# Gated multiplies on another engine, waits of GpSimd taken away, and a reordered weighting in the token mixer of a hybrid layer

## The reference, cut to what matters

```python
# one layer, SEQ = 2048 tokens, D_MODEL = 1024, 4 differential heads, 4 HGRN2 heads
proj = rms_norm(x, g) @ w_in                       # q k v | q f i g
# differential attention, swept over blocks of 128 queries, block-causal in chunks of 64
p = softmax(where(mask, q_blk @ k.T, -inf))        # two maps per head
w = p[0] - lam * p[1]
od = rms_norm(w @ v, subln_g) * (1 - lam_init)
# HGRN2, chunkwise: decayed causal scores inside a chunk, a state between chunks
o = scores @ v_c + (q_c * exp(b_c)) @ state
state = exp(b_last) * state + (k_c * exp(b_last - b_c)).T @ v_c
orr = rms_norm(o, hgrn_norm_g) * silu(g)
x = x + concat(od, orr) @ w_out
x = x + (silu(h @ w_gate) * (h @ w_up)) @ w_down   # h = rms_norm(x)
```

## Time and profile before

| | |
|---|---|
| median of 3 runs | 2812.81 us (2812.19 to 2814.52) |
| profiled execution | 2812.81 us |
| its span, first to last instruction | 2811.1 us |
| PE, PEld busy | 2643.0 us (94%), 2235.6 us (80%) |
| DVE, ACT, POOL busy | 1495.4, 1106.0, 756.8 us |
| mean granted TensorE clock | 0.973 of full |

### The profile page before, as it was taken

One profiled execution on the slowest core, in us unless ns is written; L12 is line 12 of the kernel. 1 busy time (PEld: TensorE's weight loads), 2 busy tenths in 40 slices (PEclk: granted clock), 3 DMA queues, 4 the chain that ended last, 5 costly groups with the idle time before them and its releaser, 6 DMA issues. The chain is left out here.

```text
span 2811.1 us, 34114 instructions
## 1 busy us (share of the span) xinstructions
PE 2643.0 (94%) x13384; PEld 2235.6 (80%) x13384; DVE 1495.4 (53%) x1887; ACT 1106.0 (39%) x1871; POOL 756.8 (27%) x527
## 2 busy tenths in 40 slices
PE   7999999995999999987995999999999997999999
PEld 6888888885888888875884888887888885888887
DVE  5434343431676767653336656657656554446643
ACT  4434343331567666673234222224222222423221
POOL 5000000001524242300003554455544542146400
PEclk9999999997999999998997999999999998999999
DMA  4545455455443433206656333335433333787763
GB/s 162 197 165 180 135 179 177 153 180 151 114 106 106 106 106 83 76 16 202 211 179 216 98 113 98 99 105 197 113 98 98 102 112 96 254 291 253 254 212 126
DMA packets 338672, 415.78 MB, mean 148 GB/s; under 512 B 18512, under 2 KB 212048, under 8 KB 336720
## 3 DMA queue, kind: packets, MB, share of 16 engines
q1 hardware_dynamic: 338512, 413.60, 47.1%
HBM read 291.38 MB, written 122.16 MB: 147 GB/s over the span
## 5 line engine op out<-in xcount | busy, mean ns | idle before, releaser
L1850 PE MATMUL gate_bank<-gate_b_hi,gate_a_hi 128*128 128x512 f32 x1232 | 482.8, 392 | 35.6 <-DVE first_b_lo L1730 21.6
L1852 PE MATMUL gate_bank<-gate_b_hi,gate_a_lo 128*128 128x512 f32 x1232 | 481.7, 391 | 0.0
L1851 PE MATMUL gate_bank<-gate_b_lo,gate_a_hi 128*128 128x512 f32 x1056 | 412.6, 391 | 0.0
L1850 PEld LDWEIGHTS gate_bank<-gate_b_hi,gate_a_hi 128*128 128x128 f32 x1232 | 232.9, 189 | 86.4 <-issue 22.6
L1852 PEld LDWEIGHTS gate_bank<-gate_b_hi,gate_a_lo 128*128 128x128 f32 x1232 | 232.8, 189 | 48.6
L2128 PE MATMUL down_prod<-down_w_hi,down_f_hi 128*128 128x512 f32 x616 | 241.3, 392 | 20.1 <-DVE down_f_lo L2064 19.1
L525 PE MATMUL proj_prod<-proj_w_hi,proj_h_hi 128*128 128x512 f32 x640 | 253.0, 395 | 6.8 <-DVE proj_w_lo L380 6.1
L380 DVE TENSOR_TENSOR proj_w_lo<-proj_w_raw,proj_w_hi 128x2048 fp32r<-128x2048 f32 x56 | 128.8, 2300 | 230.1 <-ACT proj_w_hi L280 230.1
L527 PE MATMUL proj_prod<-proj_w_hi,proj_h_lo 128*128 128x512 f32 x640 | 250.1, 391 | 0.0
L526 PE MATMUL proj_prod<-proj_w_lo,proj_h_hi 128*128 128x512 f32 x640 | 249.9, 390 | 0.0
L2129 PE MATMUL down_prod<-down_w_lo,down_f_hi 128*128 128x512 f32 x616 | 240.6, 391 | 0.0
(11 more groups left out here) (212 smaller groups left out, 5569.7 us busy)
## 6 DMA issues: line engine op xcount, KB each, us to landing
proj_w_raw<-in_w_in_dram SPq DMA_DIRECT2D x56, 1024.0 KB, 6.5
first_full<-in_w_gate_dram SPq DMA_DIRECT2D x88, 256.0 KB, 4.0
gate_full<-in_w_up_dram SPq DMA_DIRECT2D x88, 256.0 KB, 4.0
ff<-gate_ff_sum SPq DMA_DIRECT2D x88, 256.0 KB, 2.9
down_w_raw<-in_w_down_dram SPq DMA_DIRECT2D x22, 1024.0 KB, 7.5
down_f_raw<-ff SPq DMA_DIRECT2D x56, 384.0 KB, 3.3
down_f_raw<-ff SPq DMA_DIRECT2D x56, 320.0 KB, 3.4
gate_b_lo<-operands SPq DMA_DIRECT2D x12, 1024.0 KB, 9.8
```

The source lines that it names most:

```text
L1850: pe.matmul(dst, a_hi[:, pos, s, :], b_hi[pos][:, s, :], start=opens and s == 0, stop=False, skip_group_check=True)
L1851: pe.matmul(dst, a_hi[:, pos, s, :], b_lo[pos][:, s, :], start=False, stop=False, skip_group_check=True)
L1852: last = pe.matmul(dst, a_lo[:, pos, s, :], b_hi[pos][:, s, :], start=False, stop=s == HALF_SLABS - 1, skip_group_check=True)
```

## The change

Four places of `mix_tokens` are edited. (1) GpSimd's running products of a head are made at the head's beginning, all seven, behind the gate product of the head before. (2) GpSimd no longer waits for `combined`, neither in the levels nor in front of the gate product. (3) The recurrence's chunks 4 to 7 are normalised by VectorE, one instruction of 128x512 with a broadcast scale each, at the end of the step in which ScalarE did it; behind the last step ScalarE first normalises the attention's four chunks in a row, and then takes the chunks. (4) `behind` is gone: groups 0 and 1 are always weighed in the step in which they are turned.

```diff
-    def behind(s):
-        return 1 if groups_of(s) == 3 else 2
...
 # GpSimd
             for h in range(HEADS):
-                if h == 0:
-                    pool.wait_ge(rf_in, 16)
-                    for m in range(LEVELS):
-                        product(h, m)
+                pool.wait_ge(rf_in, 16 * (h + 1))
+                for m in range(LEVELS):
+                    ...
+                    if m:
+                        pool.wait_ge(whole_made, h * LEVELS + m)
+                    nc.gpsimd.tensor_tensor(whole[m + 1][:], src[:, :, 0], src[:, :, 1], ALU.mult).then_inc(whole_made, 1)
...
                 for m in range(LEVELS):
                     for side in range(2):
-                        n = fill_at("level", side, m)
-                        pool.wait_ge(fill_done, filled(h, n))
-                        behind_combination(h, n)
+                        pool.wait_ge(fill_done, filled(h, fill_at("level", side, m)))
...
-                if h + 1 < HEADS:
-                    pool.wait_ge(k_ready[1], (h + 1) * LEVELS)
-                    pool.wait_ge(q_ready[1], (h + 1) * UPDATES)
-                    pool.wait_ge(rf_in, 16 * (h + 2))
-                    for m in range(LEVELS - 1):
-                        product(h + 1, m)
-                    pool.wait_ge(fill_read, filled(h, len(FILLS) - 1))
-                    product(h + 1, LEVELS - 1)
-                gate(h)
+                pool.wait_ge(rgate_in, 16 * (h + 1))
+
+                pool.wait_ge(fill_read, filled(h, len(FILLS) - 1))
+                nc.gpsimd.tensor_tensor(ro[:], ro[:], rgate[:], ALU.mult).then_inc(r_gated, 1)
...
 # ScalarE: the branch of normalise() for c >= TURNS is gone (16 instructions of 128x128 a head)
                 if s == TOTAL + 1:
-                    normalise(HEADS - 1, 0)
+                    for c in range(TURNS):
+                        normalise(HEADS - 1, c)
                 for head, c in chunks_at(s):
-                    if s == TOTAL + 1 and c + 1 < CHUNKS:
-                        normalise(head, c + 1)
                     take_chunk(head, c)
                 for head, c in chunks_at(s + 1) if s < TOTAL else ():
-                    normalise(head, c)
+                    if c < TURNS:
+                        normalise(head, c)
...
 # VectorE
+            def normalise(h, c):
+                if c >= TURNS:
+                    dve.wait_ge(r_rrms_made, h + 1)
+                    dve.wait_ge(r_gated, h + 1)
+                    head = c - TURNS
+                    out = ro[:, :, head * C:(head + 1) * C]
+                    scale = ro_rrms[:].rearrange("p (c h) -> p c h", h=HEADS)[:, :, head]
+                    nc.vector.tensor_tensor(out, out, scale.unsqueeze(2).to_broadcast([P, CH, C]), ALU.mult).then_inc(r_scaled, 1)
...
+                for head, c in chunks_at(s + 1) if s <= TOTAL - 1 else chunks_at(s):
+                    normalise(head, c)
...
 # TensorE
-                    pe.wait_ge(r_scaled, (h * HEADS + c - TURNS + 1) * CH)
+                    pe.wait_ge(r_scaled, h * HEADS + c - TURNS + 1)
...
-                    for g in range(behind(s - 2), groups_of(s - 2)):
+                    for g in range(2, groups_of(s - 2)):
                         weigh(s - 2, g)
...
-                    if g < behind(s - 1):
+                    if g < 2:
                         weigh(s - 1, g)
```

More of the change, by code:

```diff
@@ L828, in _ @@
         def _(pool):
-            def product(h, m):
-                src = whole[m][:] if m else rf[:].rearrange("p h n -> p (h n)")
-                src = src.rearrange("p (n s) -> p n s", s=2)
-                if m:
-                    pool.wait_ge(whole_made, h * LEVELS + m)
-                nc.gpsimd.tensor_tensor(whole[m + 1][:], src[:, :, 0], src[:, :, 1], ALU.mult).then_inc(whole_made, 1)
-            def behind_combination(h, n):
-                step = h * STEPS + n // 2
-                if n % 2 == 0 and step:
-                    pool.wait_ge(combined, step)
-            def gate(h):
-                pool.wait_ge(rgate_in, 16 * (h + 1))
-                pool.wait_ge(fill_read, filled(h, len(FILLS) - 1))
-                if h + 1 < HEADS:
-                    pool.wait_ge(combined, (h + 1) * STEPS - 1)
-                nc.gpsimd.tensor_tensor(ro[:], ro[:], rgate[:], ALU.mult).then_inc(r_gated, 1)
-            for h in range(HEADS):
-                if h == 0:
-                    pool.wait_ge(rf_in, 16)
-                    for m in range(LEVELS):
-                        product(h, m)
+            for h in range(HEADS):
+                pool.wait_ge(rf_in, 16 * (h + 1))
+                for m in range(LEVELS):
+                    src = whole[m][:] if m else rf[:].rearrange("p h n -> p (h n)")
+                    src = src.rearrange("p (n s) -> p n s", s=2)
+                    if m:
+                        pool.wait_ge(whole_made, h * LEVELS + m)
+                    nc.gpsimd.tensor_tensor(whole[m + 1][:], src[:, :, 0], src[:, :, 1], ALU.mult).then_inc(whole_made, 1)
                 for side in range(2):
@@ L933, in normalise @@
             def normalise(h, c):
-                if c < TURNS:
-                    act.wait_ge(o_rrms_made, h + 1)
-                    for t in range(c * GROUP, (c + 1) * GROUP):
-                        nc.scalar.activation(o_all[h % 2][:, t, :], o_all[h % 2][:, t, :], ACT.Copy, scale=o_rrms[:, t:t + 1]).then_inc(o_normed, 1)
-                else:
-                    act.wait_ge(r_rrms_made, h + 1)
-                    act.wait_ge(r_gated, h + 1)
-                    head = c - TURNS
-                    for t in range(CH):
-                        part = ro[:, t, head * C:(head + 1) * C]
-                        at = t * HEADS + head
-                        nc.scalar.activation(part, part, ACT.Copy, scale=ro_rrms[:, at:at + 1]).then_inc(r_scaled, 1)
+                act.wait_ge(o_rrms_made, h + 1)
+                for t in range(c * GROUP, (c + 1) * GROUP):
+                    nc.scalar.activation(o_all[h % 2][:, t, :], o_all[h % 2][:, t, :], ACT.Copy, scale=o_rrms[:, t:t + 1]).then_inc(o_normed, 1)
             act.wait_ge(chain, 2)
```

## The result

The changed kernel takes 2838.47 us (median of 4 runs, 2837.49 to 2840.85) against 2812.5 us (2811.06 to 2814.52) for the kernel before on the same chip: a ratio of 1.0093, 95% interval 1.0076 to 1.011, some 26 us slower. The forecast was 17 us slower, 2829.8, in a range of 2816 to 2845. The direction and the range held. The 26 us lie just above the 10 to 24 to which the prediction gave 0.60, and the forecast was 9 us too low.

The account below looks back on a forecast made before the run. TensorE's order of work was taken to bound a head, other engines mattering where it stands for them. Weighing +7.2, head ends +6.6, levels +2.4, chunks +4.2, tail -3.4 summed to +17.0 us: 2829.8, range 2816 to 2845.

Parts of the forecast that it names:

- 10 to 24: Whole kernel: the forecast case, slower by this many us, chance 0.60; the forecast's own times are 2823 to 2837.
- (4) the weighing: Steps 10 to 13: 0.89 us moved ahead of the first scores, partly filling slack; 1.8 us a head, +7.2 us.
- ends of the heads: Three head ends: the early GpSimd products hold VectorE's combination, L1008 ends 2.2 us late each time; +6.6 us.
- levels, steps 7 and 8's combinations: Without its wait GpSimd's k or q can precede L1008; 0.6 us a head on the path, +2.4 us.
- chunks, steps 4 and 5, clock aside: VectorE's normalisations may stand for GpSimd's k and q and make L1008 late; +4.2 us, between 0 and 12.6.
- tail: Behind the last step: ScalarE's chain shortens, six turns of 1.15 us pacing copies; gain 3.4 us, bounds 4.9 and 1.
- The rival that it is free: Steps 10 to 13: the moved weighing costs nothing, leaving +9.8 us, 2822.6; chance 0.10.
- a lateness of all that is left of the other instruction: VectorE against GpSimd: the loser is late by the other's whole remainder; L1004 in step 9 late by 0.23 of 0.45.
- one collision a head: Steps 7 and 8: one of two close races lost per head, 0.6 us left on the path; +2.4 us.
- The rival that both hold it, 2850: Every collision is held by both k and q: levels cost 14, chunks 12.6, sum +37 us; chance 0.15.
- a third of 12.6: Chunks, ends of steps 4 and 5: share taken of the upper bound 3 x 2 x 2.1 us, giving +4.2.
- The rival in which ScalarE is the bound, 2793: ScalarE's queue, not TensorE's, sets a head's length, so 19.6 us come off; chance 0.04.

Follow-up runs that it names:

- experiment 1: Only the moved weighing, group 1 weighed in the step in which it is turned, on the kernel before: 2820.43 us, ratio 1.0024.
- experiment 2: Only the early running products and the gate product without its wait, on the kernel before; levels still wait: 2819.94 us, ratio 1.0018.
- experiment 3: Only the levels' GpSimd wait for the combination removed, on the kernel before: 2818.75 us, ratio 1.0019.
- experiment 4: Only chunks 4 to 7 normalised by VectorE, all GpSimd waits kept, on the kernel before: 2809.4 us, ratio 0.9988.
- experiment 5: The changed kernel with the levels' GpSimd wait for the combination put back: 2822.86 us, ratio 1.0035 to the kernel before.
- experiment 6: Levels without their wait and chunks on VectorE together, on the kernel before; weighing and head ends as before: 2827.9 us, ratio 1.0053.
- Experiment 8: The changed kernel plus 8 unused identity matmuls ahead of step 5's turns in heads 1 to 3: 2836.83 us, ratio 1.0086 to the kernel before.
- experiment 10: The changed kernel with each VectorE chunk normalised by 4 tensor-by-scalar instructions of 128x128 instead of one: 2842.31 us, ratio 1.0104 to the kernel before.
- experiment 11: Rerun of the kernel before with VectorE normalising the recurrence's four chunks only behind the last step: 2810.22 us, ratio 0.9989.

## Why the prediction was right and where it was off

| term | forecast | measured | from |
|---|---|---|---|
| (4) the weighing | +7.2 | +8.2 | experiment 1 |
| ends of the heads | +6.6 | +5.6 | ledger, experiment 2 |
| levels, steps 7 and 8's combinations | +2.4 | +5.7 | experiment 3 |
| chunks, steps 4 and 5, clock aside | +4.2 | +7.1 | ledger: 6.6; experiments 4 and 5: 3 x 0.15 |
| clock behind step 5's stand | none | +7.7 | ledger: 8.2 less 3 x 0.15 |
| clock behind step 9's stand | none | -4.2 | three dips of 1.4 that this execution lacks |
| tail | -3.4 | -3.8 | ledger |
| start of the mixer, steps 0 and 1 | none | +1.4 | ledger |

The measured column adds to 27.7 for a shift of 27.2; rounding and the 0.5 us that terms share at steps 8 and 9 make the rest.

**The weighing** was argued by slacks of each step: 0.34, 0.68, 0.44, 0.34 for steps 10 to 13, that is 1.8 a head. It is 2.05. The manner was right; experiment 1 has 0.4 at step 9's combination, which is made in the prediction's step 10, then 0.85, 0.74 and 0.5, and gets 0.44 back a step later, which the prediction did not have. The rival that it is free is out.

**The ends of the heads** went as written: L1004 was to stand to the end of the first product, 1.5 us, and took 1.49; L1008 was to take 3, and took 3.09; 2.2 us late, and 2.16 measured. The 0.3 us per head that came back at step 15 were not in it. That the products' departure from step 9 is worth nothing was right too: 0.67 gained and lost again (experiment 2). One reading in this part was wrong. The prediction says that the trace agrees with a lateness of all that is left of the other instruction. It does not: when L1004 came, 0.43 us of the product were left, and it was late by 0.23. In the changed kernel the held instructions fall short in the same way, by 0.2 us: 1.27 of 1.48 and 0.87 of 1.07 at the end of head 1, 0.80 of 1.00 for the 128x1024. The measurement decides; the sum, which had 2.2 and not 2.3, is not touched.

**The levels** were mis-sized. I called the races of steps 7 and 8 close and took one collision a head, of which 0.6 would be left. Both were lost, in every head, with 0.8 each. Nor did they fall one way and then the other: each came out the same in all four heads. The step that failed is "one collision a head"; that one GpSimd instruction, and not the pair, holds L1008 was right. The rival that both hold it, 2850, is out: L970 at 128x1024 is 2.08, not 2.9. What was seen in steps 3 to 6, that a combination already begun makes GpSimd wait, held too.

**The chunks** had the right mechanism and the wrong weight. That L1008 "comes behind a GpSimd that no longer waits, and is held once more: 2.1 us on the path" is what happened, 2.2 us, in step 4 of heads 1 to 3. In step 5 it did not: 0.15. The parts of the 2.2 are other ones than forecast: the prediction had 0.85 from the normalisations and the rest from one hold; measured are 0.58 (experiment 4), 0.84 for the ratio L966 behind k and 0.79 for L970 beside q. Taking a third of 12.6 for "as likely as not" gave 4.2; half, one of the two steps, would have given 6.3 for 7.1. Experiments 3, 4 and 6 show that the 1.6 us a head beyond the chunks' own 0.58 exist only when levels and chunks come together: the chunks delay VectorE by half a microsecond, and only then does the level's k, freed of its wait, get ahead of it.

**The clock** was missing from the sum altogether, and with 7.7 us it is, beside the weighing, the largest item of the measured column. The prediction read that TensorE stands 2.3 us in step 9 and did not ask what the granted clock does behind such a stand; in the heads other than the one it quoted, the trace of before had the answer, 0.50 for some 3 us. The 2.10 us stand that the collisions of step 4 made is of the same kind, and comes in three heads of three. Experiment 8 shows that it is the stand: with something to do in it, the clock stays at 1.00. It also shows that the clock's 7.7 could not be won back whole: 5.2 came back, and a new collision took the rest. That the 17 and the 26 lie so near is in part luck: the missing 7.7 stands against the -4.2 of dips that this execution does not have. Whether their absence is chance is open. In the four kernels that have both the early products and the moved weighing (the changed kernel, experiments 5, 8 and 10) the clock dips behind 2 of 16 stands of step 9, in the other eight executions in which the stand is unfilled behind 18 of 32, though the stand is 2.29 us long in all of them. No run tested why.

**The tail** was right to 0.4 us, but not by its mechanism alone: the prediction paced the last six copies by turns of 1.15 us, and the trace has turns of 0.63 to 1.1 us and copies that wait for the stores, which was only a bound of the prediction. The rival in which ScalarE is the bound, 2793, is out: ScalarE lost 19.5 us of work, and with the chunks alone (experiment 4) steps 4 and 5 became longer, not shorter. The start of the mixer, 1.4 us in the ledger, has no cause in the change that I could find: in the experiments it lies between -0.5 and 1.8, and the 1.8 are those of experiment 11, whose program there is that of the kernel before. So it is the difference of two executions.

## What to carry to other kernels

A wait that looks like an idle engine's may be what keeps two engines' instructions from meeting: before taking it away, look which instruction of the other engine it lets pass, and how often in the loop the two would come within one instruction's length, for such a race was lost here in every head that ran the same work, or in none. Two changes that each cost half a microsecond can meet: time them together and apart. And where TensorE sets the pace, a stand of 2 us is to be priced at its length and at what the clock does behind it.

## What the runs showed of the hardware that was not expected

TensorE's granted clock fell to 0.50 behind stands of 2.1 to 2.3 us in which it had nothing to do: behind the 2.29 us of step 9 in 20 of 48 cases, behind the 2.10 us of step 5 in nine of nine. It also fell behind two shorter stands close together, 1.5 and 1.3 us at the end of a head, but in only 2 of 15 cases, both in experiment 2. So the length of the stand alone does not tell whether it falls; what does is open. It stayed there for 3.4 to 10.2 us, and 1.0 to 4.3 us were lost each time. Eight matmuls of the identity in the stand, which left 0.3 to 0.5 us of it, kept it at 1.00 in each of the seven stands where they were tried in a profiled execution: the three of step 5 say much, the four of step 9 little.

The exclusion of VectorE and GpSimd goes turn by turn. At 897.24 in the changed kernel GpSimd begins k; VectorE's L970 is ready at 897.29, waits for k, and then runs ahead of q, which takes 2.03 us in place of 1.06:

```profile
897.29 2.08 DVE L970 SCALAR_TENSOR_TENSOR att_expo<-att_expo,att_ratio 128x1024 f32<-128x1024 f32 x1
...
897.24 1.05 POOL L841 TENSOR_TENSOR rec_k<-rec_k,rec_whole 128x512 f32<-128x512 f32 x1 [2.54 <-PE rec_fill L1124]
898.25 2.03 POOL L843 TENSOR_TENSOR rec_q<-rec_q,rec_whole 128x512 f32<-128x512 f32 x1
```

So a row of GpSimd instructions without a gap between them did not hold a VectorE instruction for longer than one of them, 0.8 us here and 0.87 at the end of head 1, where six products follow each other. A VectorE row of several such instructions, as the normalisations and the combination are, pays again for each GpSimd instruction that it meets: the ratio behind k and the multiply-add beside q in step 4, and in experiment 10 only the first two of eight.
